# 192 instead of 128 tokens fetch their expert rows in a PEER layer, and u is turned one quarter ahead of its lower halves

## The chip, the cores and the metric

The kernel runs on one NeuronCore of one Trainium2 chip. The metric is the device time of one execution in microseconds (us), start to end. Engines are named as in the profile: PE (TensorE), DVE (VectorE), ACT (ScalarE), POOL (GpSimd), SP (which only issues DMAs).

## What is computed

One block of a hybrid transformer on 512 tokens of width 2048, all in fp32: attention and an RWKV scan, an output projection with a layer norm, then a PEER layer, which the change is about, and a last layer norm. Cut to what matters:

```
def _peer_ffn(x, w_q, sub_keys, expert_u, expert_v):      # x: 512 x 2048
    ...                                                   # 8 heads, top 16 of 128x128 pairs of keys each
    expert_idx = jnp.take_along_axis(cand_i, best_pos, axis=-1)   # 128 of 16384 experts per token
    gate = jax.nn.softmax(best_s, axis=-1)
    def chunk(args):
        xc, ic, gc = args                                 # 128 tokens
        u = jnp.take(expert_u, ic, axis=0)                # rows of 2048 floats
        act = jax.nn.gelu(jnp.einsum('cd,cjd->cj', xc, u), approximate=False) * gc
        return jnp.einsum('cj,cjd->cd', act, jnp.take(expert_v, ic, axis=0))
```

expert_u and expert_v are 16384 x 2048 fp32 each, 128 MB each.

## The kernel before, in words

The stages run one after the other, with a barrier between them. `route` finds each token's 128 experts and gates. Then the PEER layer is computed in two ways at once, in `experts`:

- **Dense, for tokens 128 to 511** (DENSE = 384): every expert is evaluated for every token. There are 128 steps `s`, one for each block of 128 experts. A step loads the block's u (1 MB, four DMAs of 32 partitions, `load_u`), DVE turns it with a 32x32 transpose in four quarters `q` (`turn`, L2050), ACT writes the upper half of each quarter as fp32r (`u_half`) and DVE the lower half (`u_rest`, both through `split`, L95 and L96), and PE multiplies: `product` (L102) makes three fp32r matmuls (upper by upper, upper by lower, lower by upper) for each of 16 slices of the width, 48 matmuls of 128x128 by 384 columns. ACT takes Gelu, DVE multiplies by the token's gate for that expert (`gate_hidden`, L2061; the matrix of gates was made by `gate_matrix`), and upper and lower half are written to `a` (L95, L96). Four steps make a group: once its four blocks of `a` are there, their part of the output is added up in the four steps that follow, with 48 more matmuls a step whose weights are v (loaded in halves of 512 KB by `load_v`, split by ACT and, for the lower half, by POOL, `v_rest`), and DVE adds each result into `yt` (`add`, L2074). So a full step has eight PE pieces of 12 matmuls, u(q) and y(q) by turns.
- **By fetching, for tokens 0 to 127**: in each step one of the 128 choices of all 128 tokens is computed: POOL issues an indirect DMA that brings each token its row of u (1 MB, `fetch`, L2131), DVE multiplies it by x and sums (`dot`, L2079), ACT makes Gelu and gate (`choice`), a second indirect DMA brings the rows of v, and DVE adds row times number to `y_first` (`take`, L2087). The rows go through a ring of three 1 MB buffers.

The order on each engine is written out by hand in the loop over `s` and `q`. DVE in quarter q of step s: `gate_hidden(s-1)` (q = 0), `turn(s+1, q)`, the lower half of `a` (q = 0), `add`, `dot` (q = 1), `u_rest(s+1, q)`, `take` (q = 3). The split u and v stand in rings of four quarters. SP issues the loads of u, v and gates in a fixed order, each when its buffer is free.

`gate_matrix` builds the gates of the dense tokens as a matrix, four tokens to a unit: DVE compares (L1884, L1885), PE adds up (L1854), ACT copies (L1868); 96 units. `finish` turns `yt` back with PE (L2188) and makes the last layer norm, 128 tokens at a time.

## Time and profile before

| | us |
|---|---|
| median of 3 runs (5097.19 to 5101.87) | 5099.47 |
| the profiled execution | 5100.68 |
| its span, first to last instruction | 5099.0 |
| `gate_matrix`, 2606 to 2781 of the span | 175 |
| PE waits for the dense tokens' x, to 2843 | 62 |
| `experts`, 2843 to 5033 | 2190 |
| `finish`, 5033 to 5099 | 66 |

The span is that of the profile, the metric some 2 us more. A stretch of the table is found by the first and last instruction of its stage. Busy shares over the whole span mix these stages and are of little use; the rows further down are of single stages.

### The profile page before, as it was taken

How to read it: one execution, taken by the hardware profiler on the slowest of the kernel's cores; microseconds unless marked ns; L12 is line 12 of the kernel's file. 1: busy time of each engine (PE TensorE's matmuls, PEld its weight loads, DVE VectorE, ACT ScalarE, POOL GpSimd, SP SyncE). 2: the span in 40 equal slices, each digit the busy share in tenths (PEclk: the TensorE clock that was granted, in tenths of full speed). 3: DMA queues.
4: the chain of work that ended last, by engine and by line, in shares of the span. 5: the costliest groups of instructions: out<-in, count | busy, mean ns of one | idle time of the engine just before them, and what ended most of it. 6: DMA issues, size and time to landing. Idle time of an engine off the chain costs nothing. (4 is left out here: it accounts for less than half of the span.)

```text
span 5099.0 us, 60536 instructions
## 1 busy us (share of the span) xinstructions
PE 4453.5 (87%) x23108; PEld 3965.4 (78%) x23108; DVE 3163.2 (62%) x4666; ACT 1543.0 (30%) x2477; POOL 1613.2 (32%) x976
## 2 busy tenths in 40 slices
PE   8999999865766498889965599999999999999995
PEld 6888888623435487677754599999999999999995
DVE  2222222266993443469458588888888888888885
ACT  2111111134441232222322233333333333333332
POOL 0000000000452000033520255555555555555552
PEclk9999999976778799999999799999999999999997
DMA  4333333236105443234315998989888898999883
GB/s 157 115 119 123 123 123 123 79 117 149 36 19 168 157 139 143 74 121 137 120 48 159 287 260 263 262 259 261 260 260 261 260 262 262 262 261 261 261 254 128
DMA packets 556411, 909.28 MB, mean 178 GB/s; under 512 B 44680, under 2 KB 398832, under 8 KB 518928
## 3 DMA queue, kind: packets, MB, share of 16 engines
q1 hardware_dynamic: 518672, 635.62, 43.1%
q0 software_dynamic: 36864, 268.45, 16.2%
q8 instruction: 145, 2.38, 0.2%
q10 hardware_dynamic: 640, 2.10, 0.1%
q14 instruction: 90, 0.74, 0.0%
HBM read 809.51 MB, written 96.56 MB: 178 GB/s over the span
## 5 line engine op out<-in xcount | busy, mean ns | idle before, releaser
L102 PE MATMUL h_ps<-h_xs,h_ut 128*128 128x384 f32 x6144 | 1152.8, 335 | 69.0 <-DMA h_xs<-xs_d 62.1
L102 PE MATMUL h_ps<-h_a,h_v 128*128 128x384 f32 x6144 | 1154.1, 335 | 34.5 <-DVE h_a L96 34.5
L102 PEld LDWEIGHTS h_ps<-h_xs,h_ut 128*128 128x128 f32 x6144 | 1078.2, 189 | 71.3 <-DMA h_xs<-xs_d 62.3
L102 PEld LDWEIGHTS h_ps<-h_a,h_v 128*128 128x128 f32 x6144 | 1070.9, 188 | 44.7 <-DVE h_a L96 44.7
L96 POOL TENSOR_TENSOR h_v<-h_v_raw,h_v 128x512 fp32r<-128x512 f32 x512 | 766.9, 1498 | 872.0 <-ACT h_v L95 869.9
L102 PE MATMUL a_ps<-a_xt,a_w 128*128 128x512 f32 x4224 | 960.0, 390 | 7.7 <-DVE a_w L96 7.7
L102 PEld LDWEIGHTS a_ps<-a_xt,a_w 128*128 128x128 f32 x4224 | 794.6, 188 | 172.8 <-issue 7.9
L96 DVE TENSOR_TENSOR h_ut<-h_u_turn,h_ut 128x512 fp32r<-128x512 f32 x512 | 352.3, 688 | 389.9 <-ACT h_ut L95 389.6
L95 ACT ACTIVATE h_v<-h_v_raw 128x512 fp32r<-128x512 f32 x512 | 322.5, 630 | 588.4 <-PE h_ps L102 588.4
L95 ACT ACTIVATE h_ut<-h_u_turn 128x512 fp32r<-128x512 f32 x512 | 323.7, 632 | 569.9 <-PE h_ps L102 469.3
L96 DVE TENSOR_TENSOR a_w<-a_raw,a_w 128x2048 fp32r<-128x2048 f32 x88 | 201.2, 2288 | 452.9 <-issue 230.6
L2131 POOL DMA_INDIRECT h_rows<-in_peer_u,idx_first x128 | 353.4, 2761 | 239.7 <-POOLq L31 208.9
L2050 DVE STREAM_TRANSPOSE h_u_turn<-h_u_raw 128x512 f32<-128x512 f32 x512 | 359.4, 702 | 63.7 <-DMA h_u_raw<-in_peer_u 45.4
L2079 DVE CUSTOM_DVE_ANT_0 h_rows<-h_rows,h_x 128x2048 f32<-128x2048 f32 x128 | 320.5, 2504 | 0.0
L78 POOL MEMSET b_ident<- 128x128 f32 x1 | 0.2, 204 | 994.0 <-POOLq L31 994.0
L2087 DVE SCALAR_TENSOR_TENSOR y_first<-h_rows,h_acts,y_first 128x2048 f32<-128x2048 f32 x128 | 302.4, 2362 | 0.6 <-ACT h_acts L2027 0.6
L2074 DVE TENSOR_TENSOR yt<-yt,h_ps 128x384 f32<-128x384 f32 x496 | 263.9, 532 | 31.9 <-PE h_ps L102 26.9
L224 ACT COPY a_ob<-a_ps 128x512 f32<-128x512 f32 x44 | 25.8, 587 | 769.2 <-PE a_ps L102 769.2
L96 POOL TENSOR_TENSOR f_w<-f_raw,f_w 128x2048 fp32r<-128x2048 f32 (+1 forms) x36 | 157.3, 4373 | 216.2 <-ACT f_w L95 216.2
L2061 DVE TENSOR_TENSOR h_hid<-h_hid,h_gt 128x384 f32<-128x384 f32 x128 | 206.8, 1616 | 1.1 <-ACT h_hid L2015 1.1
L224 DVE COPY a_ob<-a_ps 128x512 f32<-128x512 f32 x44 | 30.4, 692 | 284.4 <-PE a_ps L102 284.4
L579 DVE TENSOR_TENSOR d_prod<-d_wt,d_at 128x1 f32<-128x1 f32 (+62 forms) x63 | 165.1, 2621 | 27.4 <-DMA d_at<-g_d 25.2
(306 smaller groups left out, 5341.4 us busy)
## 6 DMA issues: line engine op xcount, KB each, us to landing
h_u_raw<-in_peer_u SPq DMA_DIRECT2D x512, 256.0 KB
h_v_raw<-in_peer_v SPq DMA_DIRECT2D x256, 512.0 KB
a_raw<-in_w_in SPq DMA_DIRECT2D x44, 2048.0 KB
sums_d<-g_grid SPq DMA_DIRECT2D x3, 8192.0 KB
h_gt<-sums_d SPq DMA_DIRECT2D x128, 192.0 KB
proj_t<-a_ob SPq DMA_DIRECT2D x44, 512.0 KB, 2.8
o_raw<-in_w_o SPq DMA_DIRECT2D x16, 1024.0 KB, 5.0
f_raw<-in_peer_w_q SPq DMA_DIRECT2D x8, 2048.0 KB
```

Source lines behind the costliest of these rows:

```text
L78: self.step(self.pool.memset(tile, value))
L95: return act.activation(hi, whole, ACT.Copy).then_inc(done, 1)
L96: return dve.tensor_tensor(lo, whole, hi.bitcast(F32), ALU.subtract).then_inc(done, 1)
L102: mm = pe.matmul(out, lhs[a], rhs[b], start=(first and n == 0), stop=(last and n == 2))
L224: copy(ob[s // 2][:, s % 2, :], ps[:, s, :]).then_inc(out_done[odd], 1)
L579: dve.tensor_tensor(tile, wt[:, 0:t, 0:t], at[:, 0:t, t].unsqueeze(1).broadcast_to([P, t, t]), ALU.mult)\
L2050: dve.transpose(u_turn[q % 2][:, :, :].rearrange("p c (g i) -> p g c i", i=32), u_raw[s % 2][:, :, q * P:(q + 1) * P].rearrange("p g (c i) ...
L2061: dve.tensor_tensor(hid[s % 2][:, :], hid[s % 2][:, :], gt[s % 2][:, :], ALU.mult).then_inc(a_gated, 1)
L2074: dve.tensor_tensor(out, out, made, ALU.add).then_inc(y_added, 1)
L2079: dve.tensor_tensor_reduce(rows[r % RR][:, :], rows[r % RR][:, :], x1[:, :], 1.0, 0.0, ALU.mult, ALU.add, dots[:, j:j + 1]).then_inc(row_u ...
L2087: dve.scalar_tensor_tensor(y_first[:, :], rows[r % RR][:, :], acts[:, j:j + 1], y_first[:, :], ALU.mult, ALU.add).then_inc(row_used, 1)
L2131: pool.indirect_dma_start(rows[r % RR][:, :], None, table, bass.IndirectOffsetOnAxis(ap=idx_first[:, j:j + 1], axis=0))\
```

## The change

- FETCH = 192 tokens are computed by fetching. The last 64 of them (128 to 191) are done with two choices side by side: partitions 0 to 63 hold choice j, partitions 64 to 127 choice j + 64 of the same 64 tokens, so that they take 64 jobs of 128 rows. With the 128 jobs of the first 128 tokens there are JOBS = 192, three in two steps; every third is a "pair" job. The two halves of `y_pair` are added in `finish` by a matmul with a matrix `both` of two stacked identities. `route` computes indices and gates for them, and moves the second half of the heads to partitions 64 to 127 by two small DMAs.
- DENSE = 320: matmuls of 320 columns in place of 384, and narrower gates, Gelu, `a` and `add`. `gate_matrix` makes 80 units, not 96.
- The ring of fetched rows has four buffers, the rings of split u and v three quarters in place of four (WR = 3).
- DVE turns quarter n + 4 while it writes the lower half of quarter n + 3 (n counts quarters); before, turn and lower half of one quarter stood in the same slot. A block's u buffer is loaded anew after its last lower half (`u_lo`), not after its last turn.
- Blocks are taken in another order (`block_of`): the four blocks of a group are 32 blocks apart in u and v.

On DVE in the expert stage (L96 is a lower half, `h_x1...` marks a dot, `y_...` a take; the number behind a name is the buffer). Before, one step:

```order
L2061 TENSOR_TENSOR h_hid1<-h_hid1,h_gt1 128x384
L2050 STREAM_TRANSPOSE h_u_turn0<-h_u_raw1 128x4x4x32
L96 TENSOR_TENSOR h_a11<-h_hid1,h_a01 128x384
L2074 TENSOR_TENSOR yt<-yt,h_ps 128x384
L96 TENSOR_TENSOR h_ut10<-h_u_turn0,h_ut00 128x512
L2050 STREAM_TRANSPOSE h_u_turn1<-h_u_raw1 128x4x4x32
L2074 TENSOR_TENSOR yt<-yt,h_ps 128x384
L2079 ISA h_rows0,h_dots<-h_rows0,h_x1 128x2048
L2079 ISA h_dots 128x1
L96 TENSOR_TENSOR h_ut11<-h_u_turn1,h_ut01 128x512
```

And of the change, the middle of a pair of steps, quarters 0 to 2 (of 8):

```order
L2116 TENSOR_TENSOR h_hid1<-h_hid1,h_gt1 128x320
L115 STREAM_TRANSPOSE h_u_turn0<-h_u_raw1 128x4x4x32
L96 TENSOR_TENSOR h_a13<-h_hid1,h_a03 128x320
L2129 TENSOR_TENSOR yt<-yt,h_ps 128x320
L96 TENSOR_TENSOR h_ut12<-h_u_turn1,h_ut02 128x512
L2134 ISA h_rows0,h_dots<-h_rows0,h_x1_first 128x2048
...
L96 TENSOR_TENSOR h_ut11<-h_u_turn1,h_ut01 128x512
L2143 SCALAR_TENSOR_TENSOR y_first<-h_rows1,h_acts,y_first 128x2048
L2134 ISA h_rows2,h_dots<-h_rows2,h_x1_first 128x2048
```

A lower half now reads the turn buffer that was written one slot earlier (`h_u_turn1`, while the turn before it writes `h_u_turn0`), and a take and a dot can stand back to back.

On POOL, in the same place, before:

```order
L2131 DMA h_rows0<-in_peer_u,idx_first 128x2048
L96 TENSOR_TENSOR h_v11<-h_v_raw1,h_v01 128x512
L96 TENSOR_TENSOR h_v12<-h_v_raw2,h_v02 128x512
L2131 DMA h_rows1<-in_peer_v,idx_first 128x2048
L96 TENSOR_TENSOR h_v13<-h_v_raw2,h_v03 128x512
```

and of the change:

```order
L2191 DMA h_rows2<-in_peer_u,idx_pair 128x2048
L96 TENSOR_TENSOR h_v12<-h_v_raw1,h_v02 128x512
L2191 DMA h_rows3<-in_peer_v,idx_pair 128x2048
L96 TENSOR_TENSOR h_v10<-h_v_raw1,h_v00 128x512
L2191 DMA h_rows0<-in_peer_u,idx_first 128x2048
L96 TENSOR_TENSOR h_v11<-h_v_raw2,h_v01 128x512
```

POOL issues a fetch between nearly every two lower halves of v: six in eight, where there were four.

The diff, cut to its core:

```diff
 SEL = PH * TOPK
-DENSE = T - P
+FETCH = P + P // 2
+DENSE = T - FETCH
+PAIR = P // 2
...
@@ route, SP
+            sp.wait_ge(sm.sem, sm.at(0, "gate_pair1"))
+            sp.dma_start(fetch_idx[1][PAIR:P, :], late_idx[:, :]).then_inc(late_moved, 16)
+            sp.dma_start(fetch_gates[1][PAIR:P, :], late_gates[:, :]).then_inc(late_moved, 16)
+            sp.wait_ge(late_moved, 32)
...
@@ route, DVE, for each head
+                pair = late_idx if h >= PH // 2 else fetch_idx[1]
+                c.mark("index_pair", dve.scalar_tensor_tensor(
+                    pair[0:PAIR, h % (PH // 2) * TOPK:(h % (PH // 2) + 1) * TOPK], found[0][0:PAIR, 1, here],
+                    float(NKEY), found[1][0:PAIR, 1, here], ALU.mult, ALU.add))
...
@@ gate_matrix
+    SKIP = (FETCH - P) // QUAD
+    UNITS = DENSE // QUAD
...
-            for u in range(NQ * (NB - 1)):
+            for u in range(UNITS):
...
@@ experts
-    AR, RR, VR = 7, 3, 3
+    AR, RR, VR, WR = 7, 4, 3, 3
+    JOBS = SEL + PAIR
...
-        ut = [[sb(f"ut{p}{r}", [P, Q, P], F32R) for r in range(Q)] for p in range(2)]
+        ut = [[sb(f"ut{p}{r}", [P, Q, P], F32R) for r in range(WR)] for p in range(2)]
...
-        vv = expert_v.rearrange("o (g b n) (h c) -> (o g) h n b c", b=GRP, n=P, c=2 * P)
+        vv = expert_v.rearrange("o (b g n) (h c) -> (o g) h n b c", b=GRP, n=P, c=2 * P)
...
+        def block_of(s):
+            return s % GRP * GROUPS + s // GRP
+        def job(j):
+            pair = j % 3 == 2
+            return int(pair), j // 3 if pair else j // 3 * 2 + j % 3
...
             def load_u(s):
+                if s >= 2:
+                    sp.wait_ge(u_lo, Q * (s - 1))
+                b = block_of(s)
...
                     if h == 0 and s + 3 < STEPS:
-                        sp.wait_ge(u_turned, Q * (s + 2))
                         load_u(s + 3)
...
@@ ACT
-                if s >= 1:
-                    act.wait_ge(h_used, Q * (s - 1) + q + 1)
+                if n >= WR:
+                    act.wait_ge(h_used, n - WR + 1)
...
+                    at = Q * s + q
+                    if at % 8 in (1, 3, 6) and s < STEPS:
+                        choice(at // 8 * 3 + (1, 3, 6).index(at % 8))
...
@@ DVE
-                    if s + 1 < STEPS:
-                        turn(s + 1, q)
+                    t, z = divmod(Q * s + q + WR + 1, Q)
+                    if t < STEPS:
+                        turn_u(t, z)
...
-                    if q == 1 and s < SEL:
-                        dot(s)
-                    if s + 1 < STEPS:
-                        u_rest(s + 1, q)
-                    if q == 3 and s < SEL:
-                        take(s)
+                    t, z = divmod(Q * s + q + WR, Q)
+                    if t < STEPS:
+                        u_rest(t, z)
+                    if s < STEPS:
+                        m, at = divmod(Q * s + q, 8)
+                        if at in (2, 4, 7):
+                            take(3 * m + (2, 4, 7).index(at))
+                        if at in (0, 2, 5):
+                            dot(3 * m + (0, 2, 5).index(at))
...
@@ POOL
-                    if q == 0:
-                        fetch(2 * s + 2)
-                    if q == 2:
-                        fetch(2 * s + 3)
+                    m, at = divmod(Q * s + q, 8)
+                    if at in (0, 2, 3, 4, 5, 7):
+                        fetch(6 * m + (0, 2, 3, 4, 5, 7).index(at) + RR - 1)
...
@@ finish, PE
+                    if first:
+                        pe.matmul(ps[0:first, j % 8, :], both[:, :], y_pair[:, T * g:T * (g + 1)], start=True, stop=True)
```

## Rows read from the trace of the kernel before

**Rows 1.** Windows of the steady part of the expert stage; first line: columns
```profile
core 0: us, PE busy (x) PEld busy (x) DVE busy (x) ACT busy (x) POOL busy (x), PEclk, DMA share, GB/s
3000.00:4500.00 1500.00, 1483.16 (x8522) 1476.13 (x8521) 1223.30 (x1510) 556.17 (x1064) 870.27 (x534) 1.00 0.90 261
```

**Rows 2.** Timeline of PE over one step; start us, us long, idle before
```profile
3504.64 2.24 PE L102 MATMUL h_ps<-h_xs,h_ut 128*128 128x384 f32 x12
3506.72 2.24 PE L102 MATMUL h_ps<-h_a,h_v 128*128 128x384 f32 x12
...
3510.88 1.73 PE L102 MATMUL h_ps<-h_a,h_v 128*128 128x384 f32 x9
3513.37 0.79 PE L102 MATMUL h_ps<-h_a,h_v 128*128 128x384 f32 x3 [0.76 <-DVE h_a L96]
```

**Rows 3.** Groups of PE by shape, whole span
```profile
L102 PE MATMUL a_ps<-a_xt,a_w 128*128 128x512 f32 x4224 | 960.0, 390 | 7.7 <-DVE a_w L96 7.7
...
L1622 PE MATMUL f_ps<-f_keys_t,f_q 128*128 128x128 f32 x128 | 16.7, 275 | 0.0
```

**Rows 4.** Groups, 3000 to 4500 us; busy us, mean ns of one, idle before
```profile
L96 POOL TENSOR_TENSOR h_v<-h_v_raw,h_v 128x512 fp32r<-128x512 f32 x356 | 535.2, 1503 | 605.4 <-ACT h_v L95 603.8
...
L2050 DVE STREAM_TRANSPOSE h_u_turn<-h_u_raw 128x512 f32<-128x512 f32 x355 | 249.2, 702 | 0.0
L96 DVE TENSOR_TENSOR h_ut<-h_u_turn,h_ut 128x512 fp32r<-128x512 f32 x355 | 244.1, 688 | 274.2 <-ACT h_ut L95 274.2
...
L95 ACT ACTIVATE h_v<-h_v_raw 128x512 fp32r<-128x512 f32 x355 | 223.6, 630 | 403.6 <-PE h_ps L102 403.6
L2079 DVE CUSTOM_DVE_ANT_0 h_rows<-h_rows,h_x 128x2048 f32<-128x2048 f32 x89 | 223.0, 2506 | 0.0
L2087 DVE SCALAR_TENSOR_TENSOR y_first<-h_rows,h_acts,y_first 128x2048 f32<-128x2048 f32 x89 | 208.8, 2346 | 0.0
L2074 DVE TENSOR_TENSOR yt<-yt,h_ps 128x384 f32<-128x384 f32 x355 | 188.7, 531 | 3.7
L2061 DVE TENSOR_TENSOR h_hid<-h_hid,h_gt 128x384 f32<-128x384 f32 x89 | 147.1, 1652 | 0.0
L2131 POOL DMA_INDIRECT h_rows<-in_peer_v,idx_first x89 | 84.8, 953 | 13.5 <-issue 0.5
L96 DVE TENSOR_TENSOR h_a<-h_hid,h_a 128x384 fp32r<-128x384 f32 x89 | 49.7, 559 | 0.0
```

**Rows 5.** Timeline, DVE and POOL where a take meets POOL's lower half
```profile
3508.25 2.35 DVE L2087 SCALAR_TENSOR_TENSOR y_first<-h_rows,h_acts,y_first 128x2048 f32<-128x2048 f32 x1
...
3509.77 1.98 POOL L96 TENSOR_TENSOR h_v<-h_v_raw,h_v 128x512 fp32r<-128x512 f32 x1 [1.77 <-ACT h_v L95]
3510.51 1.65 DVE L2061 TENSOR_TENSOR h_hid<-h_hid,h_gt 128x384 f32<-128x384 f32 x1
```

**Rows 6.** The page's DMA queues and the number of fetches
```profile
q0 software_dynamic: 36864, 268.45, 16.2%
```

**Rows 7.** Windows of the DMA engines within a step; columns as in rows 1
```profile
3504.00:3505.00 1.00, 1.00 (x8) 1.00 (x7) 0.96 (x3) 0.10 (x1) 0.00 (x0) 1.00 1.02 418
3512.00:3514.00 2.00, 1.24 (x8) 0.92 (x7) 2.00 (x5) 1.16 (x2) 0.00 (x0) 1.00 1.04 229
3518.00:3519.00 1.00, 1.00 (x7) 1.00 (x7) 1.00 (x4) 0.56 (x1) 1.00 (x1) 1.00 0.12 37
```

**Rows 8.** Timeline: one fetch and one load of u, as they are issued
```profile
3499.04 2.83 POOL L2131 DMA_INDIRECT h_rows<-in_peer_u,idx_first  x1
...
3504.82 2.28 SPq L1936 DMA_DIRECT2D h_u_raw<-in_peer_u  x4
```

**Rows 9.** Windows of the gate matrix and of the expert stage's parts
```profile
2606.00:2781.00 175.00, 113.71 (x772) 95.42 (x770) 173.80 (x768) 56.55 (x97) 0.00 (x0) 0.98 0.34 97
2843.00:2919.00 76.00, 59.54 (x294) 57.17 (x295) 55.14 (x66) 24.21 (x48) 22.36 (x17) 0.85 0.97 269
2919.00:4997.00 2078.00, 2055.04 (x11808) 2045.46 (x11808) 1690.52 (x2084) 768.16 (x1472) 1200.69 (x736) 1.00 0.90 259
```

More of the change, by code:

```diff
@@ L103, in product, with turn_view, turn @@
     return mm
+def turn_view(expert_u):
+    return expert_u.rearrange("o (b g i) (a j) -> (o b) a i g j", g=4, i=32, a=4)
+def turn(dve, out, raw, q):
+    return dve.transpose(out.rearrange("p c (g i) -> p g c i", i=32),
+                         raw[:, :, q * P:(q + 1) * P].rearrange("p g (c i) -> p g c i", i=32))
 def project_in(nc, x, w_in, proj_t):
@@ L1482, in route @@
                    five % ((0,) * 5) + five % ((1,) * 5) + "names cand " + five % ((2,) * 5) +
-                   "shift mask float match0 match1 pick0 pick1 sum0 sum1 index")
-        sm = Steps(hd.sem, hd.end(PH), "first less sum inverse gate gate_first")
+                   "shift mask float match0 match1 pick0 pick1 sum0 sum1 index index_pair")
+        sm = Steps(hd.sem, hd.end(PH), "first less sum inverse gate gate_first gate_pair0 gate_pair1")
+        late_idx, late_gates, late_moved = sb("late_idx", [PAIR, PAIR], U32), sb("late_gates", [PAIR, PAIR]), sem("late_moved")
         exped, xs_stored = sem("exped"), sem("xs_stored")
@@ L1862, in _ @@
                 act.copy(by_choice[n][:, :, :].rearrange("p c t -> p (c t)"), ps[:, n, 0:3 * P]).then_inc(kept, 1)
-            for u in range(NQ * (NB - 1)):
-                n, v = divmod(u, NQ)
+            for u in range(UNITS):
+                n, v = divmod(u + SKIP, NQ)
                 act.wait_ge(made, u + 1)
@@ L1875, in _ @@
             dve.wait_ge(named, 1)
-            for u in range(NQ * (NB - 1)):
-                n, v = divmod(u, NQ)
+            for u in range(UNITS):
+                n, v = divmod(u + SKIP, NQ)
                 dve.wait_ge(kept, n + 1)
@@ L1913, in experts @@
         rows = [sb(f"rows{r}", [P, D]) for r in range(RR)]
-        x1 = sb("x1", [P, D])
-        dots, acts = sb("dots", [P, SEL]), sb("acts", [P, SEL])
+        x1 = [sb(f"x1_{n}", [P, D]) for n in ("first", "pair")]
+        dots, acts = sb("dots", [P, JOBS]), sb("acts", [P, JOBS])
         ps = ctx.enter_context(nc.psum_tensor("h_ps", [P, 8, T], F32))
@@ L1947, in _ @@
             load_u(1)
-            sp.dma_start(x1[:, :], x1_d[0:P, :]).then_inc(x1_in, 16)
+            sp.dma_start(x1[0][:, :], x1_d[0:P, :]).then_inc(x1_in, 16)
+            for z in range(2):
+                sp.dma_start(x1[1][z * PAIR:(z + 1) * PAIR, :], x1_d[P:FETCH, :]).then_inc(x1_in, 16)
             load_gate(0)
@@ L2026, in choice @@
                 act.wait_ge(dot_gelu, j + 1)
-                act.activation(acts[:, j:j + 1], acts[:, j:j + 1], ACT.Copy, scale=gates_first[:, j:j + 1])\
+                act.activation(acts[:, j:j + 1], acts[:, j:j + 1], ACT.Copy, scale=fetch_gates[pair][:, c:c + 1])\
                    .then_inc(dot_act, 1)
-            for q in range(Q):
+            for q in range(WR):
                 u_half(0, q)
@@ L2086, in take @@
                 dve.wait_ge(row_used, r)
-                dve.scalar_tensor_tensor(y_first[:, :], rows[r % RR][:, :], acts[:, j:j + 1], y_first[:, :],
+                dve.scalar_tensor_tensor(y[:, :], rows[r % RR][:, :], acts[:, j:j + 1], y[:, :],
                                          ALU.mult, ALU.add).then_inc(row_used, 1)
-            for q in range(Q):
-                turn(0, q)
-                if q >= 1:
-                    u_rest(0, q - 1)
-            u_rest(0, Q - 1)
-            dve.memset(y_first[:, :], 0.0).then_inc(cleared, 1)
-            dve.wait_ge(cleared, 1)
-            dve.wait_ge(x1_in, 16)
+            turn_u(0, 0)
+            for q in range(WR):
+                turn_u(0, q + 1)
+                u_rest(0, q)
+            for y in y_fetch:
+                dve.memset(y[:, :], 0.0).then_inc(cleared, 1)
+            dve.wait_ge(cleared, 2)
+            dve.wait_ge(x1_in, 48)
             for s in range(last):
@@ L2164, in _ @@
         def _(pool):
-            Setup(pool, const).identity(ident)
+            c = Setup(pool, const)
+            c.identity(ident)
+            c.fill(both[:, :], 0.0)
+            for first in (0, PAIR):
+                c.keep(both[:, :], ALU.not_equal, [[-1, PAIR]], 1, 1.0, base=-first)
+            assert c.n == 5
         @block.sync
@@ L2186, in _ @@
                         pe.wait_ge(summed, j - 6)
+                    first = FETCH - P if n == 1 else 0
+                    t = n * P - FETCH
+                    if first:
+                        pe.matmul(ps[0:first, j % 8, :], both[:, :], y_pair[:, T * g:T * (g + 1)], start=True, stop=True)
                     for i in range(4):
-                        t = pe.transpose(ps[:, j % 8, i * P:(i + 1) * P], yt[:, 4 * g + i, (n - 1) * P:n * P],
-                                         ident[:, :])
-                    t.then_inc(turned, 1)
+                        here, made = yt[:, 4 * g + i, t + first:t + P], ps[first:P, j % 8, i * P:(i + 1) * P]
+                        if first:
+                            tr = pe.matmul(made, here, ident[:, :], start=True, stop=True)
+                        else:
+                            tr = pe.transpose(made, here, ident[:, :])
+                    tr.then_inc(turned, 1)
         @block.scalar
```

138 lines of the change are left out of this document (76 added, 62 removed).

## The prediction

> **What bounds the kernel now.** I read the windows first: the change works mainly in the expert stage, and there the page's shares over the whole span say nothing. In the steady part [rows 1] PE is busy 1483 of 1500 us at a granted clock of 1.00 (the 2.4 GHz level), DVE 1223, POOL 870, ACT 556, and the DMA engines show a share of 0.90 at 261 GB/s. So PE sets the pace, but the DMA engines stand close behind and DVE next. The timeline of PE [rows 2] shows how: pieces of 12 matmuls follow one another every 2.08 us, 173.5 ns a matmul, eight pieces a step = 16.65 us, and once in four steps PE waits about 1.1 us in all for the lower half of `a` at the start of a group. A step is thus 16.9 us on average; 1500 us hold 88.7 steps. The stage's second part [rows 9] is 2078 us for 123 such steps.
>
> A gain in PE can therefore be cashed only as far as DVE, POOL and the DMA engines let it. The question is what these three need for a step.
>
> **PE after.** Matmuls of 512 columns take 960.0 / 4224 = 227 ns [rows 3], of 384 columns 173.5; that is 0.417 ns a column and 13.5 ns beside. At 320 columns: 147 ns. The smallest ones, of 128 columns, take 130 ns each on average in a short group [rows 3], so the weight load doesn't forbid 147. Bounds: 147, and 173.5 (no gain). I take 147, as it lies on a line through two measured sizes: 96 x 0.147 = 14.1 us a step, 14.4 with the group wait. PE alone would give back 2.5 us a step, 310 us.
>
> **DVE after.** Busy now 1223.3 / 88.7 = 13.8 us a step [rows 1]. Within it is time in which DVE only waits for POOL. The timeline shows it [rows 5]: the take ends at 3510.60, POOL's lower half of v (issued 3509.77) then needs until 3511.75, and the gate multiplication, 0.56 us like the other 384-column operation with two SBUF inputs [rows 4], takes 1.65. It was blocked 1.09 us. The dots show 2506 ns on average; undisturbed ones take 2.32, 0.18 is blocking. Without both, 12.5 us. The change adds half a dot and half a take a step: 0.5 x (2.32 + 2.35) = 2.3. It takes 64 columns from six operations: between 512 and 384 columns the lower halves differ by 688 - 559 = 129 ns, so 65 ns each, 0.4 together. Sum 14.4 us. Turns and lower halves are as many as before; moving the turn ahead takes away DVE's wait for ACT, 274.2 / 88.7 = 3.1 us a step [rows 4], which is what makes room for more work.
>
> To that comes POOL. It still makes four lower halves of v a step (1.29 us alone, 1503 ns on average now), and each can block a two-input DVE operation for up to 1.09 us. Turns and adds from PSUM aren't blocked: they keep 702 and 531 ns [rows 4] beside POOL. In each quarter ACT hands POOL its piece some 1.3 us after the turn (two halves of 630 ns, first u's, then v's [rows 4]), which is when DVE begins a take or dot; POOL gets in at its end. If a turn and an add follow (about 1.1 us), nothing is lost. If a second row operation follows (take then dot, once in two steps) or the gate multiplication (after the take of quarter 7), 1.09 is lost; in the three quarters without row work I count 0.1, 0.5 and 0.1. That is 2.9 in two steps, 1.45 a step. After a group's wait, ring depth 3 leaves ACT and DVE late by some 1.1 us once in four steps: 0.3. DVE: 14.4 + 1.45 + 0.3 = 16.2 us. Bounds: 14.4 (POOL wholly hidden), 14.4 + 4 x 1.09 + 0.3 = 19.1 (never hidden).
>
> The Trainium skill ("SBUF — State Buffer", section "SBUF: two separate sides") speaks against packing DVE like this: a DVE operation with two SBUF inputs and a GpSimd operation that reads SBUF exclude each other for the whole instruction. This trace agrees for rows and POOL's lower halves (blocked to 3511.75). If every one of the four met a DVE operation for its whole 1.29 us, the sum would be 14.4 + 5.2 = 19.6 instead of 16.2; the rows with undisturbed turns and adds are why I don't take that.
>
> **The DMA engines after.** This is the term that decides. Now 0.90 x 16.9 = 15.2 us a step. The fetches are the page's software queue: 16.2% of 5099 us for 256 fetches [rows 6], 3.23 us each, 6.5 us a step; the loads of u, v and gates are the other 8.7. The change adds one fetch a step (six in two steps, not four) and takes 0.1 from the gates. A fetch costs at least 1.05 MB at 418 GB/s, the rate of a window in which rows arrive [rows 7], 2.5 us; now it is 3.23; and if it runs while u is loaded, when the windows show only 229 GB/s [rows 7], 4.6. Engines that are never idle show shares of 1.02 to 1.04 [rows 7], so sums are divided by 1.04. Lowest: (8.6 + 3 x 2.5) / 1.04 = 15.5. At today's price: (8.6 + 3 x 3.23) / 1.04 = 17.6. With the added fetch at 4.6: (15.1 + 4.6) / 1.04 = 18.9. I take the middle of the first two, 16.6, as fuller queues hide the slow start of a fetch. Now the engines idle too: at 3518 they are busy 0.12 [rows 7], because the next fetch, issued while POOL was blocked by the dot (2.83 us, against 0.95 undisturbed [rows 8, 4]), hasn't started. Of 16.9 us some 2.3 are idle now; I leave 1.0, as three fetches overlap more. **A step: 17.6 us**, 0.7 more than before, with 14.4 for PE and 16.2 for DVE below it.
>
> **The sum.** 123 steady steps: +0.7 each, +86 us. The first steps [rows 9], 76 us without v and already at a DMA share of 0.97, get half a fetch each more: +6. The last four steps are 48 matmuls each without fetching: 192 x 26.5 ns = -5. `gate_matrix` is bound by DVE, 173.8 of 175 us [rows 9]; 16 of 96 units fall out: -29. The dense x is 1 MB smaller, but the x of the 64 tokens adds 1 MB behind it; PE's start: -1. Route and `finish`: two small DMAs after the last store and five short POOL and PE instructions under the first norm, +2; the new DVE operations of route stand beside PE's projections, and would cost 2 us without that cover. Together +59 on the profiled execution's 5100.7, 5160; that one stands 1.2 above the median, so I predict **5158 us**.
>
> **The rivals.**
> - *The DMA engines keep up* and the change is faster. Fetches at 2.5 us and hardly any idle time make 15.5 to 16; DVE's 16.2 then decides, with a small margin 16.3 a step: 5158 - 1.3 x 123 = 4998. For it: 418 GB/s in the pure window, deeper ring of rows. Against: u and fetches mostly overlap. It decides for faster from a step below 17.1. Chance 0.23.
> - *Balanced*, a step of 17.1 to 17.2: 5100, same. 0.07.
> - *The loads of u come late.* u's buffer is now free one slot later, leaving about 14.5 us until its first turn; now a load is issued at 3504.8 [rows 8] and four requests alone take 2.3. Behind v and beside up to three fetches (4.5 + 1.6 + 7.5 us) it doesn't fit, DVE waits, and steps take 19: 5330. 0.15.
> - *v is read more slowly*, because its four blocks now lie 32 MB apart. v's MB at the stage's 261 / 0.9 = 290 GB/s is 3.6 us; twice that makes steps of 21.2: 5600. Nothing in the trace speaks for it, since the rows of a partition group are as near as before. 0.03. The Trainium skill ("DMA: Bandwidth & Descriptors", section "Latency and other measured facts") lists halved rates for tiles whose partitions are millions of bytes apart in HBM; no run here shows it, and here partitions stay 8 KB apart.
>
> **How the numbers follow.** The forecast, 17.2 to 18.4 a step, has 0.52. Slower by over 0.2% (10 us, what a measurement of this kernel can tell from no change): 0.52 + 0.15 + 0.03 = 0.70. Same 0.07, faster 0.23. The range goes from a step of 16.8 (5060) to 18.7 (5290); about 0.2 is left outside.
>
> **What would show it.** Right: matmuls of 147 ns in pieces of 1.76 us with gaps between pieces, PE busy near 0.82 of the stage; DMA share 0.95 or more at some 300 GB/s; waits for DMA rows or u on DVE, which are absent now; hardly any DVE waits for ACT. POOL's lower halves would average over 1.5 us. `gate_matrix` near 146 us. Wrong: steps under 17 us, a DMA share under 0.93 with DVE busy throughout (then DVE and POOL bind, not the DMA engines), matmuls above 150 ns, or v's loads slower.

## The result, and the profile after

The changed kernel takes 5213.49 us (median of 4 runs, 5199.28 to 5227.19), the one before 5098.33 beside it (4 runs, 5092.96 to 5101.87): ratio 1.0227, 95% interval 1.0197 to 1.0256. It is slower by 115 us. The forecast was slower, by 60 us: 5158 in a range of 5060 to 5290. The profiled execution is the one of 5199.28, with a span of 5197.6 us, 98.6 above that of before.

Windows of the kernel after: the steady part as in [rows 1], then the first and the steady steps as in [rows 9]. Columns: PE, PEld, DVE, ACT, POOL busy us (and instructions), granted clock, DMA share, GB/s.

```profile
3000.00:4500.00 1500.00, 1254.86 (x8023) 1232.25 (x8021) 1408.86 (x1549) 508.32 (x1086) 1045.79 (x586) 0.94 1.01 302
2811.00:2896.00 85.00, 56.72 (x303) 53.88 (x303) 64.34 (x72) 24.00 (x51) 30.01 (x19) 0.83 0.98 286
2896.00:5096.00 2200.00, 1845.24 (x11805) 1810.80 (x11803) 2064.00 (x2270) 746.47 (x1597) 1534.42 (x860) 0.94 1.01 302
```

PE fell from 1483 to 1255 us of 1500, DVE rose from 1223 to 1409, POOL from 870 to 1046, and the DMA share from 0.90 to 1.01 at 302 GB/s. The 123 steady steps take 2200 us, not 2078: **17.9 us a step**, not 16.9. The first steps take 9 us more, 85 for 76. PE starts at 2811, not 2843, 32 us earlier: the gate matrix has 80 units, not 96. Together 122 + 9 - 32 = 99, the whole difference between the two executions.

Groups of the kernel after, 3000 to 4500 us (busy us, mean ns of one | idle before), which answer to [rows 4]:

```profile
L96 POOL TENSOR_TENSOR h_v<-h_v_raw,h_v 128x512 fp32r<-128x512 f32 x334 | 581.9, 1745 | 413.8 <-ACT h_v L95 411.6
L96 DVE TENSOR_TENSOR h_ut<-h_u_turn,h_ut 128x512 fp32r<-128x512 f32 x334 | 343.9, 1030 | 60.9 <-ACT h_ut L95 60.9
L2134 DVE CUSTOM_DVE_ANT_0 h_rows<-h_rows,h_x_first 128x2048 f32<-128x2048 f32 x84 | 254.7, 3032 | 0.0
L2143 DVE SCALAR_TENSOR_TENSOR y_first<-h_rows,h_acts,y_first 128x2048 f32<-128x2048 f32 x84 | 244.9, 2915 | 0.0
L115 DVE STREAM_TRANSPOSE h_u_turn<-h_u_raw 128x512 f32<-128x512 f32 x335 | 235.4, 703 | 27.8 <-DMA h_u_raw<-in_peer_u 19.0
...
L2143 DVE SCALAR_TENSOR_TENSOR y_pair<-h_rows,h_acts,y_pair 128x2048 f32<-128x2048 f32 x42 | 98.2, 2339 | 0.0
L2134 DVE CUSTOM_DVE_ANT_0 h_rows<-h_rows,h_x_pair 128x2048 f32<-128x2048 f32 x42 | 95.7, 2278 | 0.0
...
L2116 DVE TENSOR_TENSOR h_hid<-h_hid,h_gt 128x320 f32<-128x320 f32 x84 | 42.2, 503 | 0.0
```

335 turns are 83.75 steps. DVE's wait for ACT is nearly gone: 60.9 us where it was 274.2. But the lower half of u takes 1030 ns on average, where it took 688, and the dots and takes of the first 128 tokens 3032 and 2915 where those of the pair jobs, which POOL never meets, take 2278 and 2339. So DVE is blocked by POOL for 4 x 0.34 + 0.75 + 0.58 = 2.7 us a step. Busy it is for 1408.9 / 83.75 = 16.8; without the blocking 14.1; and it idles another 1.1. The gate multiplication is no longer blocked, 503 ns for 1652.

How this comes about shows the timeline (start us, us long) of DVE and POOL in the kernel after:

```profile
3509.47 1.56 POOL L96 TENSOR_TENSOR h_v<-h_v_raw,h_v 128x512 fp32r<-128x512 f32 x1 [1.20 <-ACT h_v L95]
...
3509.79 3.38 DVE L2143 SCALAR_TENSOR_TENSOR y_first<-h_rows,h_acts,y_first 128x2048 f32<-128x2048 f32 x1
...
3511.18 2.83 POOL L2191 DMA_INDIRECT h_rows<-in_peer_u,idx_first  x1 [0.15 <-issue]
...
3514.02 1.30 POOL L96 TENSOR_TENSOR h_v<-h_v_raw,h_v 128x512 fp32r<-128x512 f32 x1
3514.10 1.78 DVE L96 TENSOR_TENSOR h_ut<-h_u_turn,h_ut 128x512 fp32r<-128x512 f32 x1
```

POOL's lower half starts at 3509.47, the take 0.3 us behind it: the take lasts 3.38 us, about 1.04 more than the 2.34 of an undisturbed one. Then POOL issues a fetch beside the take, 2.83 us long, and only after it, at 3514.02, its next lower half. By then turn and add are all but over, and DVE's lower half at 3514.10 meets it and takes 1.78 for 0.68. Over the 1500 us 99 of the 334 lower halves of u are lengthened like this, to 1.77 us on average, and at 77 of them POOL's lower half stands right behind a fetch. Before, none was.

The six fetches in two steps are only part of the reason. Without the pair jobs (e7 below), with four fetches as before, the lower halves of u still average 990 ns; with all six, but turn and lower half in one slot (e8), 691; and with the turn ahead while DVE still waits for ACT (e4), 690. The three together point to the wait itself: as long as DVE waited for ACT's half of u, its own lower half began before ACT had handed POOL the next half of v. Without that wait nothing keeps the two apart. This reading is put together from the three; no run changes that alone.

The DMA engines of the kernel after, by queue over 3000 to 4500 us (packets, MB, time of the packets as a share of 16 engines):

```profile
q1 hardware_dynamic: 148214, 188.58, 54.9%
q0 software_dynamic: 36208, 263.61, 45.5%
```

and of the kernel before:

```profile
q1 hardware_dynamic: 157812, 203.93, 51.6%
q0 software_dynamic: 25488, 185.61, 38.1%
```

Per step, the fetches took 0.381 x 16.9 = 6.4 us and take 0.455 x 17.9 = 8.1, or 2.7 each for 3.2. The loads (q1) took 8.7 and take 9.8, although they carry less. The share of 1.01 stands near that of engines that never idle, 1.02 to 1.04 [rows 7].

Next, a place where u comes late, in the timeline of the kernel after (SPq is SP's issue of the loads):

```profile
3509.90 1.75 SPq L1984 DMA_DIRECT2D h_u_raw<-in_peer_u  x4
...
3523.97 0.48 DVE L2116 TENSOR_TENSOR h_hid<-h_hid,h_gt 128x320 f32<-128x320 f32 x1
...
3527.13 0.71 DVE L115 STREAM_TRANSPOSE h_u_turn<-h_u_raw 128x512 f32<-128x512 f32 x1 [2.67 <-DMA h_u_raw<-in_peer_u]
...
3527.76 0.45 DVE L96 TENSOR_TENSOR h_a<-h_hid,h_a 128x320 fp32r<-128x320 f32 x1
...
3528.27 1.17 PE L102 MATMUL h_ps<-h_a,h_v 128*128 128x320 f32 x3 [8.99 <-DVE h_a L96]
...
3529.23 3.40 PE L102 MATMUL h_ps<-h_xs,h_ut 128*128 128x320 f32 x12
```

The load took 17 us from its issue to the turn; before, one issued at 3504.8 [rows 8] was there in time and PE waited 0.76 us at its group [rows 2]. The turn stands ahead of the lower half of `a` on DVE, so a late u holds that up too, and PE with it: 9 us idle at the start of a group. Such places are rare: turns waited for u 19 of 1500 us. And most of the 9 us are there without a late u, as at an ordinary start of a group:

```profile
3240.55 1.17 PE L102 MATMUL h_ps<-h_a,h_v 128*128 128x320 f32 x3 [6.25 <-DVE h_a L96]
3241.51 3.40 PE L102 MATMUL h_ps<-h_xs,h_ut 128*128 128x320 f32 x12
```

PE waits like this at each of the 21 groups in 1500 us, 149 us in all of its 245 idle ones, because DVE's lower half of `a` comes late. Behind the wait 12 matmuls take 3.40 us for 1.92, at a granted clock of 0.50 (3240 to 3244 us). And all 42 waits of DVE for ACT's half of u, 60.9 us or 0.7 a step, stand within 10 us or so behind such a start, 1.0 and 2.0 us long as a rule. Whether PE's lower clock brings them about is not shown; no run separates it.

### The profile page after: what moved, and what is told of

It is laid out like the page before. It is cut to its first block and busy times, and to the rows that moved or that the text cites. A ratio compares the mean times of both kernels' runs of the same rounds, so it can differ in the third digit from the quotient of the medians.

```text
span 5197.6 us, 61070 instructions
## 1 busy us (share of the span) xinstructions
PE 4219.4 (81%) x23004; PEld 3711.8 (71%) x23004; DVE 3520.4 (68%) x4741; ACT 1512.3 (29%) x2589; POOL 1954.4 (38%) x1107
## 5 line engine op out<-in xcount | busy, mean ns | idle before, releaser
L102 PE MATMUL h_ps<-h_xs,h_ut 128*128 128x320 f32 x6144 | 1050.9, 323 | 217.5 <-DVE h_ut L96 153.6
L102 PE MATMUL h_ps<-h_a,h_v 128*128 128x320 f32 x6144 | 1028.0, 317 | 233.5 <-DVE h_a L96 228.4
L102 PEld LDWEIGHTS h_ps<-h_xs,h_ut 128*128 128x128 f32 x6144 | 973.5, 198 | 245.5 <-DVE h_ut L96 181.7
L102 PEld LDWEIGHTS h_ps<-h_a,h_v 128*128 128x128 f32 x6144 | 958.8, 195 | 243.0 <-DVE h_a L96 236.8
L96 POOL TENSOR_TENSOR h_v<-h_v_raw,h_v 128x512 fp32r<-128x512 f32 x512 | 889.8, 1740 | 629.4 <-ACT h_v L95 625.8
L96 DVE TENSOR_TENSOR h_ut<-h_u_turn,h_ut 128x512 fp32r<-128x512 f32 x512 | 517.1, 1010 | 90.3 <-ACT h_ut L95 89.4
L96 DVE TENSOR_TENSOR a_w<-a_raw,a_w 128x2048 fp32r<-128x2048 f32 x88 | 201.2, 2288 | 452.6 <-issue 230.6
L2134 DVE CUSTOM_DVE_ANT_0 h_rows<-h_rows,h_x_first 128x2048 f32<-128x2048 f32 x128 | 382.8, 2990 | 0.0
L2191 POOL DMA_INDIRECT h_rows<-in_peer_u,idx_first x128 | 242.7, 1896 | 201.7 <-POOLq L31 180.2
L2129 DVE TENSOR_TENSOR yt<-yt,h_ps 128x320 f32<-128x320 f32 x496 | 226.4, 457 | 24.5 <-PE h_ps L102 24.0
L96 POOL TENSOR_TENSOR f_w<-f_raw,f_w 128x2048 fp32r<-128x2048 f32 (+1 forms) x36 | 157.4, 4374 | 216.3 <-ACT f_w L95 216.3
L2191 POOL DMA_INDIRECT h_rows<-in_peer_v,idx_first x128 | 197.2, 1540 | 29.8 <-issue 13.8
```

What stands on the lines that cost most here:

```text
L96: return dve.tensor_tensor(lo, whole, hi.bitcast(F32), ALU.subtract).then_inc(done, 1)
L102: mm = pe.matmul(out, lhs[a], rhs[b], start=(first and n == 0), stop=(last and n == 2))
L2129: dve.tensor_tensor(out, out, made, ALU.add).then_inc(y_added, 1)
L2134: dve.tensor_tensor_reduce(rows[r % RR][:, :], rows[r % RR][:, :], x1[job(j)[0]][:, :], 1.0, 0.0, ALU.mult, ALU.add, dots[:, j:j + 1]).the ...
L2191: pool.indirect_dma_start(rows[r % RR][:, :], None, v_rows if r % 2 else u_rows, bass.IndirectOffsetOnAxis(ap=fetch_idx[pair][:, c:c + 1], ...
```

## The experiments

Two theories stood against one another. **A**, the forecast's: the DMA engines set 17.9 us, DVE stands below. **B**: DVE with its waits for POOL sets it, and the DMA share of 1.01 is only a queue that is always full. A third, **C**: the blocks of v 32 MB apart. The rows above fit each. All runs were compared with the kernel before on the same chip, and ratios are given against it; that of the changed kernel is 1.0227.

### Half of each block of u (e1_half_u)

```diff
-                for z in range(4):
+                for z in range(4 if s < 2 else 2):
...
-                dve.wait_ge(u_in[s % 2], 64 * (s // 2 + 1))
+                dve.wait_ge(u_in[s % 2], 64 + 32 * (s // 2))
```

> The changed kernel, but from the third block on only two of the four DMAs of each u block are issued (partitions 0 to 63; the others keep old data): 0.52 MB less a step, all engines' work the same. Two theories of the changed kernel's 17.9 us a step (5213 us). A: the DMA engines bind (share 1.01 at 302 GB/s in its steady part). Then up to 2.3 us a step of transfer goes, DVE's 16.8 us of busy time decides, and the time falls by about 1.1 x 123 = 135 us, to some 5080. B: DVE and POOL bind, since each blocks the other. Then only DVE's direct waits for u go (19 us in 1500, 0.23 a step): 5185, and the DMA share falls to some 0.90.

5196.72 us (5193.81 to 5198.56), ratio 1.0189 (1.0172 to 1.0206).

```profile
3000.00:4500.00 1500.00, 1253.92 (x8029) 1231.83 (x8028) 1424.07 (x1553) 509.74 (x1092) 1049.85 (x587) 0.95 0.88 273
```

```profile
L115 DVE STREAM_TRANSPOSE h_u_turn<-h_u_raw 128x512 f32<-128x512 f32 x336 | 236.1, 703 | 8.8
```

The DMA share fell from 1.01 to 0.88, and the step stayed: 336 turns in 1500 us are 17.9 us. DVE is busy 1424, and neither its turns nor ACT's halves of v wait for a DMA any more. So with the DMA engines relieved, DVE and POOL, with the waits for ACT, need 17.9 by themselves. A, which expected 5080, is out as the only limit; B's 5185 lies within 12 us.

### Half of POOL's work on v (e2_pool_half)

```diff
-                split(nc.scalar, nc.gpsimd, "lo", v_raw[hv % VR][:, :, (q % 2) * P:(q % 2 + 1) * P],
-                      v[0][y % WR][:, :, :], v[1][y % WR][:, :, :], v_lo)
+                n = GRP if y < WR else GRP // 2
+                split(nc.scalar, nc.gpsimd, "lo", v_raw[hv % VR][:, 0:n, (q % 2) * P:(q % 2 + 1) * P],
+                      v[0][y % WR][:, 0:n, :], v[1][y % WR][:, 0:n, :], v_lo)
```

> The changed kernel, but POOL makes the lower halves of v for only two of a quarter's four blocks (the rest keeps old data), so that an instruction of 1.29 us alone becomes some 0.7; DMA traffic the same. DVE loses 2.7 us a step to POOL in the changed kernel: lower halves of u 1030 ns instead of 684, dots 3032 instead of 2283, takes 2915 instead of 2340. B (DVE and POOL bind): about half of it goes, 1.35 x 123 = 165 us, to 5050. A (the DMA engines bind): within 25 us of 5213, with DVE waiting for DMAs instead.

5198.16 us (5184.91 to 5205.73), ratio 1.0196 (1.0179 to 1.0213). Window, and the groups that changed:

```profile
3000.00:4500.00 1500.00, 1263.29 (x8122) 1241.74 (x8121) 1272.92 (x1561) 521.52 (x1099) 795.99 (x594) 0.92 1.03 305
```

```profile
L96 DVE TENSOR_TENSOR h_ut<-h_u_turn,h_ut 128x512 fp32r<-128x512 f32 x337 | 260.9, 774 | 72.2 <-ACT h_ut L95 72.1
L115 DVE STREAM_TRANSPOSE h_u_turn<-h_u_raw 128x512 f32<-128x512 f32 x337 | 237.7, 705 | 138.7 <-DMA h_u_raw<-in_peer_u 129.8
...
L95 ACT ACTIVATE h_v<-h_v_raw 128x512 fp32r<-128x512 f32 x338 | 211.9, 627 | 485.7 <-DMA h_v_raw<-in_peer_v 281.6 <-PE h_ps L102 203.8 <-issue 0.3
```

DVE is busy 136 us less, and again the step hardly moves: 337 turns, 17.8 us. What was blocking became waiting: for u 129.8 us, where it was 19.0, and ACT for v 281.6, where it was 59.8. The DMA share is 1.03. B, which expected 5050, is out as the only limit as well.

### Both halves together (e5_both_half)

The edits of e1 and e2 in one kernel.

> Both cuts at once: half of each u block isn't loaded and POOL's lower halves of v cover two of four blocks. Each alone gave some 15 us (5197, 5198). New theory C: two limits lie at the same height in the changed kernel, DVE with POOL (17.92 us a step, exactly periodic, when the DMA load is cut) and the DMA engines (about 17.8, DVE waiting for u and ACT for v, when POOL's work is cut). C expects that both cuts together give what neither gave: DVE 16.8 - 1.35 = 15.4 with a few waits, a step of some 15.8, 5213 - 2.1 x 123 = 4955. If instead a third thing binds at 17.8 (the wait chain PE, ACT, DVE over the three-quarter rings), it stays above 5170.

4987.38 us (4978.44 to 4988.36), ratio 0.9770 (0.9754 to 0.9787).

```profile
3000.00:4500.00 1500.00, 1364.04 (x8871) 1357.46 (x8869) 1418.52 (x1714) 574.20 (x1203) 941.32 (x650) 0.95 0.99 302
```

(In this expectation and in those of e7, e8 and e10, C is the new theory of two level limits, not the spacing of the blocks.) This is what settles it. Against the changed kernel, one relief gives 0.4% and the other 0.3%, whose intervals touch its own; both give 4.6% of the time of before, 233 us, where the expectation had 258. **Two limits stand at the same height**, and neither shows until the other is gone. The rival that the expectation names, a chain of waits over the rings of three, would have kept it above 5170. Steps are 16.2 us (371 turns), with DVE busy 1418 us and the DMA share at 0.99: at the shorter step both are nearly full again.

### The blocks in their old order (e3_old_blocks), and that with half of POOL's work (e6_old_blocks_pool_half)

```diff
-        vv = expert_v.rearrange("o (b g n) (h c) -> (o g) h n b c", b=GRP, n=P, c=2 * P)
+        vv = expert_v.rearrange("o (g b n) (h c) -> (o g) h n b c", b=GRP, n=P, c=2 * P)
...
-            return s % GRP * GROUPS + s // GRP
+            return s
```

> The changed kernel with the blocks in their old order (block s in step s, a group's four blocks next to each other in u and v). A and B: no difference beyond 15 us of 5213. The rival of the prediction that v is read more slowly when its blocks lie 32 MB apart: faster than 5213 by as much as this costs; v's 1 KB packets would be visibly shorter.

5202.38 us (5200.78 to 5202.56), ratio 1.0198 (1.0181 to 1.0215). Its queues over the same 1500 us:

```profile
q1 hardware_dynamic: 148730, 189.16, 50.0%
q0 software_dynamic: 36203, 263.69, 45.2%
```

The loads cost 50.0% and not 54.9%, so 0.9 us less a step for the same bytes, and the time stays within what the intervals leave open, since DVE and POOL hold the step. Read one by one in the trace, the packets of v (1 KB) fall from 67 to 59 ns on average, those of u (2 KB) from 156 to 144. C alone is out, but the order of the blocks does burden the DMA engines. e6 asks what that is worth when they decide alone:

> POOL's lower halves cut as in the run with 5198 us, and the old block order, in which the DMA share at the same traffic was 0.96 instead of 1.01. If that share is real transfer time (v's 1 KB packets take longer when its blocks lie 32 MB apart), the DMA-bound step falls by 5% of 17.8, 0.9 us: 5198 - 110 = 5090. If block order only changes how packets are counted, within 20 us of 5198.

5145.94 us (5134.03 to 5171.14), ratio 1.0099 (1.0065 to 1.0132): 0.97% of the time of before, or 50 us, below e2. So the spacing of the blocks was part of the DMA limit, 0.4 us a step of it, half of the 0.9 that the expectation took from the share.

### The changes of order without the added tokens (e4_reorder_only)

128 tokens by fetching and 384 columns as before, with the turn ahead, rings of three for split u and v, three buffers of rows as before, the block order of the change:

```diff
-FETCH = P + P // 2
-DENSE = T - FETCH
+DENSE = T - P
...
-                        if at in (2, 4, 7):
-                            take(3 * m + (2, 4, 7).index(at))
-                        if at in (0, 2, 5):
-                            dot(3 * m + (0, 2, 5).index(at))
+                    if q == 1 and s < SEL:
+                        dot(s)
+                    if q == 3 and s < SEL:
+                        take(s)
```

> The kernel before with only the new order: 128 tokens fetched, 384 columns, three row buffers, but turns one quarter ahead, rings of three quarters, u's buffer freed after its last lower half, blocks 32 apart. PE binds before at 16.65 us a step, so A and B alike expect 5098 within 10 us, and DVE's wait for ACT's halves (274 us in 1500) mostly gone. If the shorter rings cost PE something beyond the group wait (1.1 us once in four steps), up to 0.3 us a step: 5135.

5097.01 us (10 runs, 5091.15 to 5100.82), ratio 0.9993 (0.9983 to 1.0002).

```profile
3000.00:4500.00 1500.00, 1482.21 (x8516) 1475.18 (x8516) 1214.96 (x1511) 551.95 (x1065) 765.37 (x532) 1.00 0.94 261
```

```profile
L96 DVE TENSOR_TENSOR h_ut<-h_u_turn,h_ut 128x512 fp32r<-128x512 f32 x355 | 245.1, 690 | 263.0 <-ACT h_ut L95 263.0
```

PE is back at 1482 of 1500: where PE sets the pace, turning ahead gains nothing and costs nothing. One half of the expectation failed, and the prediction had said the same: DVE's wait for ACT was to be mostly gone, and it is 263.0 us for 274.2. ACT itself waits 342 us for PE there. So the 3.1 us a step that the prediction counted as taken away by the earlier turn were mostly time in which DVE was ahead of PE. But the DMA share is 0.94 for 0.90 at the same 261 GB/s. Its queue of loads shows 57.8% where the kernel before shows 51.6%, 1.05 us a step for the same bytes, which agrees with e3 in a kernel with other limits, though more than the order of the blocks differs here.

### Without the pair jobs (e7_no_pair_jobs)

```diff
+                if j % 3 == 2:
+                    return
```

at the head of `choice`, `dot`, `take` and `fetch`, with the jobs counted anew.

> The changed kernel without the 64 pair jobs (no fetch, dot, choice or take for tokens 128 to 191, whose output is left out): 320 columns, 128 jobs in 128 steps' slots. PE's floor is 14.4 us a step, DVE's 12.1 of its own and some 2 of blocking, the DMA engines' about 15. C expects a step of 15 to 15.5: 5213 - 2.7 x 123 = 4880. So the pair jobs would cost some 330 us, while the 64 columns they save are worth at most 310.

4939.59 us (4927.68 to 4948.24), ratio 0.9675 (0.9659 to 0.9691).

```profile
3000.00:4500.00 1500.00, 1375.16 (x8988) 1357.65 (x8989) 1332.96 (x1594) 561.56 (x1125) 913.59 (x562) 0.97 0.94 274
```

The pair jobs cost 1.0227 - 0.9675 = 5.5% of the time of before, 281 us; the 64 columns that they save, with all the rest, bring 3.25% = 166. That is the change in one line. The expectation put this kernel lower, at 4880: even without the pair jobs PE is busy only 1375 of 1500. DVE and POOL still meet (POOL's lower halves average 1629 ns, and those of u are as follows), and turns wait 86 us for u.

```profile
L96 DVE TENSOR_TENSOR h_ut<-h_u_turn,h_ut 128x512 fp32r<-128x512 f32 x375 | 371.1, 990 | 46.7 <-ACT h_ut L95 46.6
```

### Turn and lower half in the same slot again (e8_same_slot)

```diff
-            turn_u(0, 0)
...
-                turn_u(0, q + 1)
+                turn_u(0, q)
...
-                    t, z = divmod(Q * s + q + WR + 1, Q)
+                    t, z = divmod(Q * s + q + WR, Q)
```

> The changed kernel with the turn in the same slot as its own lower half again, as before the change (rings of three). DVE then waits in every quarter for ACT's half of the quarter just turned, 0.63 us and the way there, about 0.75 x 4 = 3 us a step less what now are waits anyway (0.7): C expects +2 x 123 = +250, 5460. If POOL fills these waits (it gets the port while DVE waits), clearly less: some 5300.

5313.99 us (5309.07 to 5315.70), ratio 1.0418 (1.0400 to 1.0435).

```profile
L96 DVE TENSOR_TENSOR h_ut<-h_u_turn,h_ut 128x512 fp32r<-128x512 f32 x320 | 221.0, 691 | 124.5 <-ACT h_ut L95 124.5
```

With 192 tokens the turn ahead is worth 1.9%, 97 us; with 128 tokens nothing (e4). DVE waits for ACT 124.5 us instead of 60.9. The lower half of u is undisturbed here, 691 ns, but the blocking moved to the dots and takes: 3400 and 3384 ns in the pair jobs, for 2278 and 2339. The step is 18.75 us (320 turns). Of the two expectations, 5460 and some 5300 if POOL fills DVE's waits, the second came true: POOL's lower halves average 1417 ns for 1745.

### u over all 128 partitions (e9_pool_half_u_128)

On top of e2, four loads of 128 partitions each in place of four of 32:

```diff
-                    sp.dma_start(u_raw[s % 2][32 * z:32 * z + 32, :].rearrange("p (g f) -> p g f", g=4), uv[b, z])\
-                      .then_inc(u_in[s % 2], 16)
+                    sp.dma_start(u_raw[s % 2][:, T * z:T * (z + 1)], uv[b, :, :, z, :]).then_inc(u_in[s % 2], 16)
```

> The kernel with POOL's lower halves of v cut (5198 us, bound by the DMA engines) and u's block loaded by four DMAs that each cover all 128 partitions (one of the four groups of 32 experts each) instead of 32 partitions each. Same bytes, same 2 KB packets. In the changed kernel u's packets take 156 ns in the median and 84 at best, and windows in which u is loaded show some 200 to 230 GB/s against 400 with rows. If 32 partitions are what limits them, 2 us a step go, and with POOL's cut the time falls to where both cuts were, 4987 us or a little above; the DMA share falls under 0.95. If it is u's layout in HBM or anything else, it stays within 30 us of 5198.

5991.48 us (5990.68 to 6001.02), ratio 1.1756 (1.1736 to 1.1776). The window, the wait for u (us in total, times, longest) and one issue on SP's queue:

```profile
3000.00:4500.00 1500.00, 990.23 (x6029) 977.52 (x6028) 928.60 (x1166) 393.53 (x819) 590.77 (x440) 0.81 0.72 227
```

```profile
DVE h_u_turn L115 <- DMA h_u_raw<-in_peer_u: 516.2, 63, 17.1
```

```profile
3496.92 11.39 SPq L1987 DMA_DIRECT2D h_gt<-sums_d  x1
3508.36 0.58 SPq L1991 DMA_DIRECT2D h_v_raw<-in_peer_v  x1
```

Neither 4987 nor 5198: a miss, and an instructive one. The packets did get shorter: read one by one in the trace, those of 2 KB took 84 ns in the median, where those of e2 took 155 and those of the kernel after 156. Yet DVE waits 516 of 1500 us for u, and the DMA engines idle: share 0.72. Where the time goes shows SP's queue: issuing one load of gates, 0.5 us in the median in the kernel after and 0.9 in e2, holds it for 11.4 us here (5.6 in the median of 62), and the loads behind it start that much later.

The trace doesn't tell packets of one engine from another's, but it shows how many are under way at once. Of u's 2 KB packets it is 3.2 on average while any is, and five or fewer for 99% of that time; in e2 it is 8.5, and up to 22. So u came over few engines at a time: its packets are under way 958 of 1500 us, 15 us a step, for 786 in e2. The edit changed more than the partitions. The outermost dimension of the source of one load is 4 (`uv[b, :, :, z, :]`), where it was 32 (`uv[b, z]`). That this sets the number of engines fits, but no run here varies it alone. What e9 was to test, whether 32 partitions limit the load of u, it therefore doesn't answer.

### 160 tokens by fetching (e10_fetch160), and that with the loads of e9 (e11_fetch160_u_128)

A quarter in place of a half (four choices side by side for 32 tokens), matmuls of 352 columns, five jobs in four steps, three buffers of rows, the blocks in their old order:

```diff
-FETCH = P + P // 2
+FETCH = P + P // 4
...
-            pair = j % 3 == 2
-            return int(pair), j // 3 if pair else j // 3 * 2 + j % 3
+            pair = j % 5 == 4
+            return int(pair), j // 5 if pair else j // 5 * 4 + j % 5
```

> A point between the two kernels: 160 tokens fetch, the last 32 with four choices side by side (32 more jobs, five in four steps), 352 columns, three row buffers, the old block order, the new slots. PE's floor is 96 x 160.2 ns = 15.4 and 0.3 for the group wait; DVE 13.4 of its own and 2.2 blocked; the DMA engines (15.2 + 0.25 x 3.2) / 1.04 = 15.4. Theory C (two limits just above PE): all three near 15.7, a step of 16.3 for what they lose to each other: 5098 - 0.6 x 123 - 14 for gate_matrix = 5010, faster than both kernels. If three equal limits add up worse, at 16.9 a step, 5085.

5106.15 us (10 runs, 5091.99 to 5122.20), ratio 1.0013 (1.0000 to 1.0026): as before, not better, and above both times of the expectation, 5010 and 5085.

```profile
3000.00:4500.00 1500.00, 1407.07 (x8459) 1400.71 (x8458) 1328.31 (x1563) 549.67 (x1101) 963.66 (x574) 0.96 0.96 289
```

Nothing is full here, PE 1407, DVE 1328, DMA 0.96, and still the gain is gone. The waits are many and short: turns 17.1 us for u, ACT 46.5 for v, dots and takes 67 for their rows from a ring of three. My reading, which no run of its own shows, is that three limits so near one another cost more than the highest alone.

> The same with u loaded by DMAs over all 128 partitions. If that shortens u's transfer, the DMA engines leave the three limits: some 20 to 40 us below the 160-token kernel. If not, within 15 us of it.

5918.12 us (5910.42 to 5921.99), ratio 1.1609 (1.1590 to 1.1629). Expected were times near e10's; it is the same failure as e9 with other limits around it, DMA share 0.68, and again five or fewer of u's packets at once for 99% of the time in which any is. No version tried that computes the whole output beats the kernel before.

## Why the prediction was right, and where it was not

**PE: right.** Pieces of 12 matmuls follow every 1.76 us in undisturbed places, as here in the timeline of the kernel after:

```profile
3044.64 1.92 PE L102 MATMUL h_ps<-h_a,h_v 128*128 128x320 f32 x12
3046.40 1.92 PE L102 MATMUL h_ps<-h_xs,h_ut 128*128 128x320 f32 x12
3048.16 1.92 PE L102 MATMUL h_ps<-h_a,h_v 128*128 128x320 f32 x12
```

That is 147 ns a matmul, the value on the line through 512 and 384 columns. PE could have gained 310 us; it idles instead, busy 0.84 of the stage, where 0.82 was said. What the prediction left out is the clock: PE is busy 1254.9 / 83.75 = 15.0 us a step, not 14.1, since the pieces behind each group's wait run at a granted clock of 0.50 (3.40 for 1.92 us). With 17.9 us a step PE has room for that.

**Outside the steady steps: right.** PE starts 32 us earlier (30 forecast: 29 and 1); the first steps +9 for +6; the last part, 35 us to the end of the experts and 66 of `finish`, is within a few us of before. `gate_matrix` runs from 2602 to 2748, the 146 us that were said.

**The step: 17.9 us, forecast 17.6, in the bracket of 17.2 to 18.4.** This 0.3 us is 37 us over 123 steps, nearly all that lies between the 5160 forecast for a profiled execution and its 5199. (That execution is the fastest of four; the median is 14 us above it, and no trace shows these. So the slowdown, forecast at 60 us, came out at 99 in the trace and 115 in the medians.) But the step is made up otherwise than the prediction said. *"with 14.4 for PE and 16.2 for DVE below it"* is the step of the working that failed: DVE is not below, it is level.

- DVE's own work was well sized, 14.1 for 14.4. The blocking by POOL was not: 2.7 us a step for the 1.45 counted. The prediction reckoned with one loss of 1.09 a step behind takes, half of it at the gate multiplication, and with 0.1 to 0.5 in the quarters without row work, because there a lower half of v would fall under turn and add. The gate multiplication is free (503 ns); 1.4 us a step are lost at the lower halves of u, which it took for all but safe, and 1.3 at dots and takes. It left out that POOL's fetch stands ahead of its lower half, and, in this part of its working, that a fetch issued while a dot or take runs lasts 2.83 us (101 of 251 do), though it names that figure for the DMA engines. And it counted DVE's wait for ACT as gone without asking what that wait had kept apart. To this come 1.1 us of idle time for 0.3, of which 0.7 are the waits for ACT behind each group's start.
- The DMA engines' term came near (17.6, and about 17.8 where they hold the step, e2) by luck in part, through errors that offset one another. The fetches cost 2.7 us each; the 16.6 taken implied (16.6 x 1.04 - 8.6) / 3 = 2.9. The loads cost 9.8, not 8.6, and by e3, with e4 in agreement, 0.9 or so of the added 1.2 is the spacing of the blocks. The 1.0 us left for idle engines was about 0.5 (share 1.01 against 1.04).
- So *"this is the term that decides"* was half of the truth. e1 takes load from the DMA engines, and the step stays; e2 takes it from POOL, and it stays; e5 takes both, and 1.7 us a step go.

**The rivals.** *The DMA engines keep up* would have needed DVE at 16.2; it stood at 17.9 (e1), so relieved DMA engines don't make the change faster. *u's loads come late* is there as a place (2.67 us at 3527) but 19 us of 1500; it grows to 130 as soon as POOL is lighter (e2). *v is read more slowly* was given 0.03 with *"Nothing in the trace speaks for it"*. Its mechanism is real, its price was not: the loads take some 1 us a step more, not the 3.6 of a v read at half the rate, which costs some 15 us or less by the medians, within the intervals, where DVE and POOL stand as high (e3) and some 50 where they don't (e6 against e2). The Trainium skill ("DMA: Bandwidth & Descriptors", section "Latency and other measured facts") lists lower rates for tiles whose partitions are far apart in HBM. Here the partitions stay 8 KB apart and only the four blocks within a partition's row lie 32 MB apart, and the 1 KB packets of v took 73 ns on average (e4) for 50: the direction is the same here, outside the case that the Trainium skill names, at a smaller price.

**The whole-instruction lock.** A take that begins 0.3 us behind POOL's lower half is longer by 1.04 us, and a lower half of u that begins 0.08 behind it by 1.1. The Trainium skill ("SBUF — State Buffer", section "SBUF: two separate sides") has the two exclude each other for a whole instruction, and at the places shown the trace agrees. What this section of the Trainium skill doesn't decide is how often they meet: never was 14.4, always 19.6, and the runs show about half, 2.7 of 5.2 us.

**What it would show, against what it showed.** DMA share at least 0.95 at some 300 GB/s: 1.01 at 302. POOL's lower halves over 1.5 us: 1.75. Hardly any wait of DVE for ACT: 0.7 us a step for 3.1. Waits of DVE for u: 19 us, few; for rows: none, and the ring of four was deep enough. Its sign for DVE and POOL as the limit, a DMA share under 0.93, would have missed them here: the share was 1.01 with both limits level.

## What to carry to other kernels

Work moved off the engine that sets the pace buys only the distance to the next limit; size every other resource with its blocking and its waits, not by busy time, since DVE's own 14.1 us stood for 17.9. A full DMA share next to a full engine doesn't tell which one binds: relieve each by itself and then both, because two level limits hide each other (0.4% and 0.3% alone, 4.6% together). When instructions are added to a queue such as POOL's, ask what moves back behind them and what it then collides with. When a wait is taken out, ask what it had kept apart: the blocking that DVE had been spared while it waited for ACT came back as 1.4 us a step.
